# A weight ring of 16 units, a router by ranks among pairs, and a scatter in float32r halves

## The chip, the cores and the metric

The kernel runs on one core of a Trainium2 chip. The metric is the time of one execution on the device in microseconds (us); lower is better. Two kernels are compared by the medians of their runs.

## The reference

The program is a trunk of two post-norm layers on 256 tokens of width 1024. Each layer has a sub-layer of three parallel attention mixers and then a channel mixer: a dense SwiGLU in layer 0, and in layer 1 a mixture of eight experts of which each token uses two. The change is in layer 1's channel mixer:

```python
def swiglu(h, w_gate, w_up, w_down):
    return (jax.nn.silu(h @ w_gate) * (h @ w_up)) @ w_down

def moe_ffn(h, w_router, b_router, w_gate, w_up, w_down):
    """Top-2-of-8 SwiGLU experts; softmax over the two selected router logits."""
    B, S, D = h.shape
    hf = h.reshape(B * S, D)
    logits = (hf @ w_router).astype(jnp.float32) + b_router.astype(jnp.float32)
    top_v, top_i = lax.top_k(logits, TOP_K)
    top_w = jax.nn.softmax(top_v, axis=-1)
    combine = jnp.sum(jax.nn.one_hot(top_i, N_EXPERTS, dtype=jnp.float32) * top_w[..., None], axis=1)
    combine = combine.astype(h.dtype)
    out = jnp.zeros_like(hf)
    for e in range(N_EXPERTS):
        out = out + combine[:, e:e + 1] * swiglu(hf, w_gate[e], w_up[e], w_down[e])
    return out.reshape(B, S, D)
...
        h = layer_norm(ALPHA * h + y, ln_ffn_g[l], ln_ffn_b[l])
```

Everything is float32. D_FF is 3584, so an expert has three matrices of 1024 x 3584.

## The kernel before

**Weights as a stream of units.** All weights are laid out as units of 128 x 2048 float32 (1 MB). Layer 0 and 1 have 36 units each for the mixers, an expert (and the dense channel mixer) has 42. SyncE issues one load after another into a ring of slots, each when the unit that was in the slot has been used (semaphore `s_used`, counted up by TensorE at the last product of a unit). In the mixers and the dense part the ring has 7 slots (`raw_a`). In the expert part it has 14: `raw_a`, `raw_w` (one slot) and `raw_b` (six slots), whose space the mixers have used till then. `MOE_BASE` is the number of the first expert unit.

**Products in three parts.** Where many tokens are computed, a float32 product is made of three float32r products: ScalarE writes the unit's rounded copy `w_hi` (float32r), VectorE subtracts it from the unit (`w_lo`, called `lo_a`, `lo_b` and `lo_w` in the rows, in place of the raw unit), and TensorE adds up `x_hi w_hi + x_hi w_lo + x_lo w_hi` (L1530 to L1532). ScalarE and VectorE call this a split of the unit; three slots of `w_hi` are in use in the expert part. A unit needs twelve such products of 512 columns when 128 tokens are computed.

**Items.** The router lists items: an expert with up to 128 of its tokens (big, "B") or with up to 64 (small, "S"), in the order BSBSBSBS, so that experts with many tokens get the big ones. A small item takes full float32 products straight from the raw units (`x_small`, L1873 and L1907), with no split. The first seven items are written out, the eighth is the body of a loop that runs once or more often, where items overflow. Every item takes the 42 units in the order gate and up (groups of up to 1024 columns of D_FF) and down.

Each item goes like this on TensorE: the gate products of group 0 (four units); then `scatter` of the item before; up; group 1's gate; the transposes of the hidden values (L1880), and so on; near the end `gather` for the next item (L1836: 32 products that pick the tokens' columns of h by a one-hot matrix `gath`), and the last two down units. The result of an item stands in PSUM banks 4 and 5 (128 tokens x 1024). ScalarE and VectorE copy one half each to `d_sb`, four float32 products (L1847) with the transposed one-hot matrix `scat` place the rows at their tokens in banks 4 to 7, and VectorE multiplies by the router weight and adds to `cat`, which holds ALPHA * h (L1301).

**Order on an engine** is the order in which the code is written; every engine has its own instruction stream, with semaphores between them.

**The router.** After the last mixer's output h is normalised tile by tile (two tiles of 128 tokens; L1010 and L1015 are the last steps), each tile is transposed on TensorE (L1560), copied (`x_rt`), and multiplied with the router weights (L1959). `keep_warm(n)` puts n transposes of the identity matrix (L1566) on TensorE that nobody reads. VectorE finds the largest logit of each token, masks it, and finds the second (L1434 to L1446). TensorE counts ranks of tokens within experts with a triangular matrix (L1965 to L1969), VectorE makes the first gather matrix (L1312), and then the weights of the softmax, the lists of items and their overflow (L1456 to L1508). L987 are splits of units in the router's stretch, L1328 those of items.

## Time and profile before

| | us |
|---|---|
| median of 3 runs | 1654.53 (1654.35 to 1659.11) |
| the profiled execution, its own time | 1653.32 |
| its span, first to last instruction | 1651.5 |
| PE (TensorE) busy | 1557.0 (94%) |
| DVE (VectorE) busy | 963.3 (58%) |
| ACT (ScalarE) busy | 738.5 (45%) |

The mean granted TensorE clock was 0.973 of full speed. The mixers and the dense part fill the first 770 us, the router lies from 770 to 795, the eight items end at 1633, and the last normalisation and the stores of the output close the span. Durations of products overlap, since matmuls are pipelined: a product of 0.39 us can begin 0.23 us after the one before it. A row's time in the second place is that of a whole merged group where it has a count (x8).

### The profile page before, as it was taken

The page shows a single profiled execution, that of the slowest core. Times are in us where ns is not written, and L with a number is a line of the kernel's source. Part 1 is how long each engine was busy: PE and PEld are TensorE (multiplying, and loading weights), DVE is VectorE, ACT ScalarE, POOL GpSimd, SP SyncE. Part 2 cuts the span into 40 slices and gives each one's busy share as a digit, 9 for nine tenths or more (in the row PEclk, how much of TensorE's full clock was granted, in tenths as well). Part 3 has the DMA queues.
Part 4 walks back from the last instruction along what each step waited for, and adds up shares of the span by engine and source line. Part 5 has one row for each costly group of instructions (what it writes and reads, how often), then busy time and mean ns, then how long its engine had stood idle before and what let it go on. Part 6 is the DMA issues. An engine that isn't in the chain of part 4 may idle for free.

```text
span 1651.5 us, 18668 instructions
## 1 busy us (share of the span) xinstructions
PE 1557.0 (94%) x7600; PEld 1140.1 (69%) x7600; DVE 963.3 (58%) x904; ACT 738.5 (45%) x678; POOL 40.2 (2%) x30
## 2 busy tenths in 40 slices
PE   5999888999998999979899999999999999999996
PEld 3977777788886887867788436885368853688633
DVE  5547667455556546666899206993069930599403
ACT  3356654333433446653577105771057720477201
POOL 0000040000000000031000000000000000000000
PEclk9998989999999998989999999999999999999998
DMA  8353254455552452246699999999999999999994
GB/s 306 118 204 115 89 194 163 161 196 178 181 199 104 145 213 103 80 175 252 268 367 374 356 426 425 426 426 397 427 425 426 425 400 426 426 425 426 412 425 190
DMA packets 67013, 473.76 MB, mean 287 GB/s; under 512 B 8064, under 2 KB 8192, under 8 KB 10096
## 3 DMA queue, kind: packets, MB, share of 16 engines
q1 hardware_dynamic: 66096, 467.95, 70.9%
q0 software_dynamic: 832, 4.63, 0.8%
q8 instruction: 60, 0.98, 0.2%
q14 instruction: 25, 0.20, 0.0%
HBM read 471.50 MB, written 1.05 MB: 286 GB/s over the span
## 4 chain that ended last, share of the span: by engine, by line
PE 80%; DVE 9%; DMA 5%; ACT 3%; issue 2%; POOL 1%; SPq 0%; DVEq 0%; ACTq 0%; POOLq 0%
PE ps L1530 20%; PE ps L1531 19%; PE ps L1532 19%; PE ps L1873 11%; DMA raw_a<-in_w_item 4%; PE ps L1907 3%; DVE lo_a L987 2%; PE ps L1847 2%; PE ps L1836 1%; PE ps L1880 1%; ACT w_hi L662 1%; PE ps L1696 1%; PE ps L1560 1%; DMA raw_a<-in_w_mix 1%; DVE small L1003 1%
## 5 line engine op out<-in xcount | busy, mean ns | idle before, releaser
L987 DVE TENSOR_TENSOR lo_a<-raw_a,w_hi 128x2048 fp32r<-128x2048 f32 (+2 forms) x117 | 252.2, 2160 | 199.1 <-ACT w_hi L662 198.1
L662 ACT ACTIVATE w_hi<-raw_a 128x2048 fp32r<-128x2048 f32 (+2 forms) x117 | 209.5, 1796 | 180.0 <-PE ps L1532 174.5
L1530 PE MATMUL ps<-w_hi,act_hi 128*128 128x512 f32 (+1 forms) x640 | 254.8, 398 | 24.3 <-DVE act_lo L1053 11.4
L1531 PE MATMUL ps<-lo_a,act_hi 128*128 128x512 f32 (+1 forms) x640 | 249.8, 390 | 0.0
L1532 PE MATMUL ps<-w_hi,act_lo 128*128 128x512 f32 (+1 forms) x640 | 249.2, 389 | 0.0
L1328 DVE TENSOR_TENSOR lo_a<-raw_a,w_hi 128x2048 fp32r<-128x2048 f32 x81 | 184.3, 2289 | 19.7 <-ACT w_hi L898 18.8
L1530 PE MATMUL ps<-w_hi,x_hi 128*128 128x512 f32 x448 | 177.5, 396 | 9.0 <-DVE lo_a L1328 7.2
L898 ACT ACTIVATE w_hi<-raw_a 128x2048 fp32r<-128x2048 f32 x81 | 155.4, 1918 | 62.5 <-PE ps L1532 58.0
L1328 DVE TENSOR_TENSOR lo_b<-raw_b,w_hi 128x2048 fp32r<-128x2048 f32 x72 | 164.4, 2289 | 21.0 <-ACT w_hi L898 21.0
L1532 PE MATMUL ps<-w_hi,x_lo 128*128 128x512 f32 x448 | 174.6, 390 | 0.0
L898 ACT ACTIVATE w_hi<-raw_b 128x2048 fp32r<-128x2048 f32 x72 | 138.6, 1925 | 52.8 <-PE ps L1532 52.8
L1530 PEld LDWEIGHTS ps<-w_hi,act_hi 128*128 128x128 f32 x640 | 125.0, 195 | 53.3 <-DVE lo_a L987 8.6
L1532 PEld LDWEIGHTS ps<-w_hi,act_lo 128*128 128x128 f32 x640 | 125.0, 195 | 24.8
L1531 PEld LDWEIGHTS ps<-lo_a,act_hi 128*128 128x128 f32 x640 | 125.3, 196 | 22.8
L918 ACT ACTIVATE hidT<-ps 128x512 f32<-128x512 f32 (+1 forms) x16 | 8.7, 545 | 219.3 <-PE ps L1880 219.3
L1530 PEld LDWEIGHTS ps<-w_hi,x_hi 128*128 128x128 f32 x448 | 84.2, 188 | 30.8 <-issue 8.9
L1532 PEld LDWEIGHTS ps<-w_hi,x_lo 128*128 128x128 f32 x448 | 84.1, 188 | 18.2
L1873 PE MATMUL ps<-raw_a,x_small 128*64 128x512 f32 (+1 forms) x512 | 93.6, 515 | 0.0
L1530 PE MATMUL ps<-w_hi,hid_hi 128*128 128x512 f32 x224 | 87.6, 391 | 0.0
L1532 PE MATMUL ps<-w_hi,hid_lo 128*128 128x512 f32 x224 | 87.3, 390 | 0.0
L1338 DVE TENSOR_TENSOR sig<-ps,sig 128x512 f32<-128x512 f32 (+1 forms) x16 | 9.9, 619 | 128.6 <-ACT sig L909 128.6
L1873 PE MATMUL ps<-raw_b,x_small 128*64 128x512 f32 x384 | 84.6, 593 | 0.0
(254 smaller groups left out, 2228.9 us busy)
## 6 DMA issues: line engine op xcount, KB each, us to landing
raw_a<-in_w_item SPq DMA_DIRECT2D x210, 1024.0 KB, 11.4
raw_b<-in_w_item SPq DMA_DIRECT2D x144, 1024.0 KB, 14.7
raw_a<-in_w_mix SPq DMA_DIRECT2D x60, 1024.0 KB, 4.9
raw_w<-in_w_item SPq DMA_DIRECT2D x24, 1024.0 KB, 15.5
raw_a<-in_w_mix SPq DMA_DIRECT2D x8, 512.0 KB, 3.8
ln_gb<-in_ln_mix POOLq DMA_DIRECT2D x2, 1024.0 KB, 5.0
cst<-in_consts SPq DMA_DIRECT2D x1, 1178.0 KB, 20.1
h<-in_x SPq DMA_DIRECT2D x2, 512.0 KB, 8.0
```

Of the source, the lines that this page charges most:

```text
L662: nc.scalar.activation(w_hi[:, HI_SLOT[g], 0:n], raw(slot)[:, 0:n], ACT.Copy).then_inc(s_hi, 1)
L898: nc.scalar.activation(w_hi[:, it.hi_slot(k), :], raw(slot), ACT.Copy).then_inc(s_hi, 1)
L987: nc.vector.tensor_tensor(w_lo(slot)[:, 0:n], raw(slot)[:, 0:n], w_hi[:, HI_SLOT[g], 0:n].bitcast(F32), ALU.subtract).then_inc(s_lo, 1)
L1003: link(nc.vector.bn_stats(bst[:, t, b, :], src[:, t, 512 * b:512 * b + 512]))
L1328: nc.vector.tensor_tensor(w_lo(slot), raw(slot), w_hi[:, it.hi_slot(k), :].bitcast(F32), ALU.subtract).then_inc(s_lo, 1)
L1530: nc.tensor.matmul(dst, xh, wh, start=start, stop=False)
L1531: nc.tensor.matmul(dst, xh, wl, start=False, stop=False)
L1532: return nc.tensor.matmul(dst, xl, wh, start=False, stop=stop)
L1560: ins = nc.tensor.transpose(ps[:, bank, b * P:b * P + P], src[:, t, o:o + P], ident)
L1847: nc.tensor.matmul(ps[:, bank, :], scat[:, t, :], d_sb[:, 512 * half:512 * half + 512], start=True, stop=True).then_inc(s_cb, 1)
L1873: ins = nc.tensor.matmul(ps[64 * b:64 * b + 64, bank, 0:width // 2], x_small[:, kt, :], raw(slot)[:, o:o + width // 2], start=kt == 0, sto ...
L1907: ins = nc.tensor.matmul(ps[64 * half:64 * half + 64, 4 + half, :], hidT[:, b % (blocks // 2), a:a + 64], raw(slot)[:, o:o + 512], start=f ...
```

## The change

- **Ring.** `SLOTS` goes from 14 to 16: `raw_b` gets eight slots, counted down from the top of the memory, and their space comes from moving `cst`, `cat` and the small tiles. The load into the last slot waits for the last use of the layer-norm parameters `ln_gb`, which lie there. The looped eighth item uses 14 slots (`LOOP_SLOTS`).
- **Router.** The two largest logits are found by comparing all pairs: `ahead` counts for each expert how many logits are ahead of it, ties by the lower index; an expert is chosen if fewer than 2 are. The lists of items are made by operations over all values at once (`vals`, `tab`) and no longer one value at a time, in five pieces (`lists`) that stand between the splits of item 0. Two splits of units move from the router's chain to behind the gather matrix. The scaling of h into `cat` moves from VectorE to ScalarE. The first gather goes to banks 4 and 5, and item 0 begins its first products when the left half of the tokens is there.
- **Fillers.** `keep_warm` of 30 and 20 behind the two tiles become 14 and 8.
- **Scatter.** `d_sb` is replaced by `d_hi` (ScalarE, both halves, float32r) and `d_lo` (VectorE, the difference), and each bank is the sum of two float32r products.

```diff
-SLOTS_A, SLOTS = 7, 14
+SLOTS_A, SLOTS = 7, 16
+
+LOOP_SLOTS = 14
...
                     sp.wait_ge(s_used, MOE_BASE)
+                    if slot == SLOTS - 1:
+
+                        sp.wait_ge(s_lnd, 2 * DEPTH)
...
-                    hold(sp, s_used, j * ITEM_UNITS + (LOOP_BASE + k - SLOTS + 1))
+                    hold(sp, s_used, j * ITEM_UNITS + (LOOP_BASE + k - LOOP_SLOTS + 1))
...
-            def copy_down_left(it):
+            def copy_down_hi(it):
                 act.wait_ge(s_used, it.unit(ITEM_UNITS))
-                nc.scalar.activation(d_sb[:, 0:512], ps[:, 4, :], ACT.Copy).then_inc(s_dA, 1)
+                for half in range(2):
+                    nc.scalar.activation(d_hi[:, 512 * half:512 * half + 512], ps[:, 4 + half, :], ACT.Copy).then_inc(s_dA, 1)
...
             copy_tokens(0, True)
+            nc.scalar.activation(cat[:], h[:], ACT.Copy, scale=ALPHA).then_inc(s_res, 1)
...
                     norm(3, h, ln_gb, (s_gb, 48), adds, router_copy)
-                    split(nb + U_OUT + 5)
...
-            def copy_down_right(it):
-                dve.wait_ge(s_used, it.unit(ITEM_UNITS))
-                nc.vector.tensor_copy(d_sb[:, 512:1024], ps[:, 5, :]).then_inc(s_dV, 1)
+            def copy_down_lo(it):
+                for half in range(2):
+                    cols = slice(512 * half, 512 * half + 512)
+                    dve.wait_ge(s_dA, it.n * 2 + (half + 1))
+                    nc.vector.tensor_tensor(d_lo[:, cols], ps[:, 4 + half, :], d_hi[:, cols].bitcast(F32), ALU.subtract).then_inc(s_dV, 1)
...
-            first_largest(lg, m1, oh1)
-            link(nc.vector.scalar_tensor_tensor(lg2, oh1, -3e38, lg, ALU.mult, ALU.add))
-            first_largest(lg2, m2, oh2)
-            nc.vector.tensor_tensor(sel, oh1, oh2, ALU.add).then_inc(s_sel, 1)
-            nc.vector.tensor_tensor(dd, m2, m1, ALU.subtract).then_inc(s_rd, 1)
-            split(MOE_BASE + 2)
+            nc.vector.tensor_tensor(pair_gt, other, own, ALU.is_gt)
+            link(nc.vector.tensor_tensor(pair_eq, other, own, ALU.is_equal))
+            link(nc.vector.tensor_tensor(pair_eq, pair_eq, lower, ALU.mult))
+            link(nc.vector.tensor_tensor(pair_gt, pair_gt, pair_eq, ALU.add))
+            link(nc.vector.tensor_reduce(ahead, pair_gt, AX, ALU.add))
+            link(nc.vector.tensor_scalar(sel, ahead, 1.5, None, ALU.is_lt))
+            dve.sem_inc(s_sel, 1)
...
             link(nc.vector.tensor_tensor(rkm, ps[:, 6, 0:TILES * N_EXP].rearrange("p (t e) -> p t e", t=TILES), sel, ALU.mult))
-            link(nc.vector.tensor_scalar(rkm, rkm, -1.0, None, ALU.add))
             gather_matrix(lambda t: rkm[:, t, 0:1], True)
             nc.vector.tensor_copy(cnt, ps[:, 7, 0:N_EXP])
-            nc.vector.tensor_scalar(cat[:], h[:], ALPHA, None, ALU.mult)
...
+            split(MOE_BASE + 1)
             tokens_lo(0, None)
...
+            split(MOE_BASE + 2)
...
+            def by_position():
+
+                e688 = [P, 6, N_EXP, N_EXP]
+                each = prod.rearrange("p (r a b) -> p r a b", r=6, a=N_EXP)
+                link(nc.vector.tensor_tensor(each, at_pos.unsqueeze(1).to_broadcast(e688), vals.unsqueeze(2).to_broadcast(e688), ALU.mult))
+                link(nc.vector.tensor_reduce(tab[:, :, 0:N_EXP], each, AX, ALU.add))
...
-            item(Item(0), None, 3)
+            item(Item(0), None, 3, (weights, positions, by_position, overflow, overflow_items))
...
             def scatter(n):
 
-                pe.wait_ge(s_dA, n + 1)
-                pe.wait_ge(s_dV, n + 1)
                 pe.wait_ge(s_sTe, n + 1)
+
+                pe.wait_ge(s_dV, n * 2 + 2)
                 for q, bank in enumerate(SCATTER_BANKS):
                     t, half = q // 2, q % 2
-                    nc.tensor.matmul(ps[:, bank, :], scat[:, t, :], d_sb[:, 512 * half:512 * half + 512],
-                                     start=True, stop=True).then_inc(s_cb, 1)
+                    cols = slice(512 * half, 512 * half + 512)
+                    nc.tensor.matmul(ps[:, bank, :], scat[:, t, :], d_hi[:, cols], start=True, stop=False)
+                    nc.tensor.matmul(ps[:, bank, :], scat[:, t, :], d_lo[:, cols], start=False, stop=True).then_inc(s_cb, 1)
...
-                pe.wait_ge(s_xh, it.n * 2 + 2)
-                if it.big:
-                    pe.wait_ge(s_xl, it.bigs * 2 + 2)
-                project(0, GROUP_GATE[0], 0)
+                def gathered(b):
+                    pe.wait_ge(s_xh, it.n * 2 + b + 1)
+                    if it.big:
+                        pe.wait_ge(s_xl, it.bigs * 2 + b + 1)
+
+                first = before is None
+                gathered(0 if first else 1)
+                project(0, GROUP_GATE[0], 0, gathered if first else None)
...
-                keep_warm((30, 20)[t])
+                keep_warm((14, 8)[t])
```

The instruction order on TensorE (PE) from the first tile's router products to the first gather, before:

```order
L1959 MATMUL ps<-w_rt,x_rt 128x8 x8
L1566 MATMUL ps<-cst 128x128 x30
L1560 MATMUL ps<-cst,h 128x128 x8
L1959 MATMUL ps<-w_rt,x_rt 128x8 x8
L1566 MATMUL ps<-cst 128x128 x20
L1965 MATMUL ps<-rt,cst 128x8
```

The same place now, where L1619 is `keep_warm`, L1613 the transposes and L2019 the router products:

```order
L2019 MATMUL ps<-w_rt,x_rt 128x8 x8
L1619 MATMUL ps<-cst 128x128 x14
L1613 MATMUL ps<-cst,h 128x128 x8
L2019 MATMUL ps<-w_rt,x_rt 128x8 x8
L1619 MATMUL ps<-cst 128x128 x8
L2025 MATMUL ps<-rt,cst 128x8
```

The order is the same, and 16 and 12 fillers fewer stand behind the two tiles.

On VectorE (DVE), from the end of the choice of experts to the first work after the gather matrix (`gath`), before:

```order
L1446 TENSOR_TENSOR rt<-rt 128x16
L1447 TENSOR_TENSOR rt<-rt 128x2
L987 TENSOR_TENSOR lo_a<-raw_a,w_hi 128x2048
L1450 TENSOR_TENSOR rt<-ps,rt 128x16
L1451 TENSOR_SCALAR rt<-rt 128x16
L1312 TENSOR_SCALAR gath<-cst,rt 128x128 x2
L1453 COPY rt<-ps 128x8
L1454 TENSOR_SCALAR cat<-h 128x2048
```

And now (L1353 is the gather matrix, L1026 a split, L1369 an item's split, L1348 the second part of the gathered tokens):

```order
L1502 TENSOR_TENSOR rt<-rt 128x16
L1503 TENSOR_REDUCE rt<-rt 128x2
L1505 TENSOR_TENSOR rt<-ps,rt 128x16
L1353 TENSOR_SCALAR gath<-cst,rt 128x128 x2
L1507 COPY rt<-ps 128x8
L1026 TENSOR_TENSOR lo_a<-raw_a,w_hi 128x2048
L1348 TENSOR_TENSOR x_lo<-ps,x_hi 128x512 x2
L1026 TENSOR_TENSOR lo_a<-raw_a,w_hi 128x2048
L1369 TENSOR_TENSOR lo_a<-raw_a,w_hi 128x2048 x3
L1515 TENSOR_SCALAR rt<-rt 128x2
```

The splits stand behind the gather matrix, the scaling of `cat` is gone, and the first piece of the lists (from L1515) comes after three splits of the item.

On TensorE at the first scatter, that of item 0 within the small item 1, before:

```order
L1873 MATMUL ps<-raw_a,x_small 64x512 x16
L1847 MATMUL ps<-d_sb,scat 128x512 x4
L1873 MATMUL ps<-raw_a,x_small 64x512 x12
```

And now, with L1929 for the small item's products:

```order
L1929 MATMUL ps<-raw_b,x_small 64x512 x16
L1901 MATMUL ps<-d_hi,scat 128x512
L1902 MATMUL ps<-d_lo,scat 128x512
L1901 MATMUL ps<-d_hi,scat 128x512
L1902 MATMUL ps<-d_lo,scat 128x512
L1901 MATMUL ps<-d_hi,scat 128x512
L1902 MATMUL ps<-d_lo,scat 128x512
L1901 MATMUL ps<-d_hi,scat 128x512
L1902 MATMUL ps<-d_lo,scat 128x512
L1929 MATMUL ps<-raw_b,x_small 64x512 x8
```

Eight products stand where four stood, at the same place of the item; the unit ahead of them is in another slot of the ring.

## Rows read from the trace of the kernel before

**Rows 1.** The page: busy time and share of each engine.

```profile
PE 1557.0 (94%) x7600; PEld 1140.1 (69%) x7600; DVE 963.3 (58%) x904; ACT 738.5 (45%) x678; POOL 40.2 (2%) x30
```

**Rows 2.** Busy times by stretch, item 2 (big), item 3 (small); last clock, DMA share, GB/s.

```profile
1004.60:1121.10 116.50, 116.50 (x521) 94.90 (x521) 106.68 (x59) 83.39 (x50) 0.00 (x0) 1.00 1.01 426
...
1130.10:1211.00 80.90, 80.90 (x419) 32.29 (x420) 11.26 (x19) 7.16 (x13) 0.00 (x0) 1.00 1.00 416
```

**Rows 3.** Chain of waits, pieces in order of time: start, us, what.

```profile
1121.06 3.52 PE ps L1836 x32
...
1137.14 3.63 PE ps L1847 x8
...
1185.73 24.40 DMA raw_a<-in_w_item
...
1215.00 0.23 PE ps L1531
...
1225.70 3.43 PE ps L1847 x8
...
1424.71 0.47 PE ps L1530
```

**Rows 4.** Timeline at the start of item 4: start, us, instruction, [idle before].

```profile
1210.15 1.91 ACT L898 ACTIVATE w_hi<-raw_a 128x2048 fp32r<-128x2048 f32 x1 [0.39 <-DMA raw_a<-in_w_item]
...
1214.54 0.47 PE L1530 MATMUL ps<-w_hi,x_hi 128*128 128x512 f32 x1 [1.82 <-DVE lo_a L1328]
```

**Rows 5.** Timeline of SyncE's issues of loads around the router.

```profile
798.59 18.58 SPq L570 DMA_DIRECT2D raw_a<-in_w_item  x7
```

**Rows 6.** Timeline of TensorE in the router.

```profile
773.01 6.03 PE L1566 MATMUL ps<-cst 128*128 128x128 f32 x30
778.88 1.04 PE L1560 MATMUL ps<-cst,h 128*128 128x128 f32 x8
...
786.87 1.07 PE L1566 MATMUL ps<-cst 128*128 128x128 f32 x8
788.81 5.31 PE L1836 MATMUL ps<-gath,h 128*128 128x128 f32 x32 [0.87 <-DVE gath L1312]
795.59 0.47 PE L1530 MATMUL ps<-w_hi,x_hi 128*128 128x512 f32 x1 [1.46 <-ACT x_hi L883]
```

**Rows 7.** Timeline of VectorE in the router.

```profile
774.43 1.41 DVE L1015 SCALAR_TENSOR_TENSOR h<-h,small,ln_gb 128x512 f32<-128x512 f32 x2
...
782.97 0.18 DVE L1434 TENSOR_TENSOR rt<-ps,small 128x16 f32<-128x16 f32 x1
...
785.66 2.29 DVE L987 TENSOR_TENSOR lo_a<-raw_a,w_hi 128x2048 fp32r<-128x2048 f32 x1
787.86 0.17 DVE L1450 TENSOR_TENSOR rt<-ps,rt 128x16 f32<-128x16 f32 x1
...
788.28 0.48 DVE L1312 TENSOR_SCALAR gath<-cst,rt 128x128 f32<-128x128 f32 x2
...
803.17 0.17 DVE L1508 CAST itab<-rt 128x13 int32<-128x13 f32 x1
```

**Rows 8.** Timeline of VectorE in item 4: the split of unit 7.

```profile
1233.93 2.29 DVE L1328 TENSOR_TENSOR lo_w<-raw_w,w_hi 128x2048 fp32r<-128x2048 f32 x1
```

**Rows 9.** Timeline after the last item.

```profile
1632.79 0.60 ACT L876 ACTIVATE d_sb<-ps 128x512 f32<-128x512 f32 x1 [1.70 <-PE ps L1907]
...
1633.59 3.67 PE L1847 MATMUL ps<-d_sb,scat 128*128 128x512 f32 x8 [0.84 <-ACT d_sb L876]
1634.83 1.50 DVE L1301 SCALAR_TENSOR_TENSOR cat<-ps,rt,cat 128x512 f32<-128x512 f32 x2 [1.34 <-PE ps L1847]
1636.55 1.50 DVE L1301 SCALAR_TENSOR_TENSOR cat<-ps,rt,cat 128x512 f32<-128x512 f32 x2 [0.22 <-PE ps L1847]
```

**Rows 10.** Stretches of the router: length, busy times, granted clock, DMA share, GB/s.

```profile
774.00:776.00 2.00, 2.00 (x11) 2.00 (x10) 1.74 (x5) 0.00 (x0) 0.00 (x0) 0.50 1.02 430
788.50:792.00 3.50, 3.19 (x15) 3.19 (x16) 3.19 (x14) 0.00 (x0) 0.00 (x0) 0.51 0.37 152
```

255 lines of the change are left out of this document (139 added, 116 removed).

## The prediction

> **What bounds the kernel now.** I read the page first for the shares of the engines. TensorE is busy for 94% of the span, VectorE for 58% [rows 1], so the first question is what keeps TensorE's work as long as it is. The change works in the second half, in the router and the eight expert items. Two limits close together must be told apart, so I asked for the busy times of one big and one small item [rows 2]. The reader is to see that TensorE is busy in all 116.5 us of the big item and all 80.9 us of the small one, while the DMA engines are at a share of 1.0 too and move 426 and 416 GB/s.
>
> The chain of waits says which one holds [rows 3]. A pair of items (big and small) lies between the first products at 1214.54 [rows 4] and at 1424.71, so a pair takes 210.2 us. It has 84 weight units of 1.049 MB; at 426 GB/s a unit is 2.46 us and a pair 206.8 us. The chain runs over products of TensorE, and once in each pair over the landing of a load that was issued 24.4 us earlier. What that landing costs is in the timeline [rows 4]: ScalarE waited 0.39 us for the unit before it could split it, and TensorE stood still 1.82 us while ScalarE and VectorE split it. The other 1.4 us would be there with the unit landed long before. So TensorE's own work sets the pace, with the DMA 3 us behind it. A saved microsecond of TensorE work in an item is a saved microsecond of the kernel, until the DMA's limit is met.
>
> The second place is the router. The ring was full and the DMA ran dry soon after 788.5 [rows 10]; the next load was issued at 798.59, when TensorE had used its first expert unit [rows 5]. Everything between the end of the normalisation and the first expert product is a serial chain of small steps [rows 6, 7].
>
> **The change part by part.**
>
> *Router, on the path.* The second tile of h is normalised at 774.43 + 1.41 = 775.84 [rows 7], but its transposes began at 778.88: TensorE was in the 30 filler transposes, 6.03 us at 0.20 us each [rows 6]. With 14 they end at 773.01 + 2.8 = 775.8, which frees 3.0 us. The 8 real transposes, 1.04 us where they stood, now begin at the fillers' slow pace (8 x 0.20 = 1.6 us), so 0.6 goes back: **2.4 us**. The choice of two experts was 13 small operations, from 782.97 to the start of the next split at 785.66, 0.21 us each. It becomes seven, four of them on 128 elements instead of 16. Those have no row; the bounds are 0.17 us (16 elements) and 0.60 us (a quarter more than the 0.48 us that two 128-element operations took at 788.28). At about 0.35 us the chain is 2.1 us: **0.6 us**. The rank products were done when TensorE went on to 8 fillers at 786.87 [rows 6], but VectorE read them at 787.86, since it was in the split of 2.29 us that began at 785.66. That split and the one before it move behind the gather matrix, and one operation of 0.21 us goes, so the matrix is done 1.1 us earlier. The fillers end at 786.87 + 1.07 = 787.94, and the gather, which began at 788.81, can't start ahead of that: **0.8 us**. The first product waits for half of the gathered tokens instead of all. TensorE stood still 1.46 us before it [rows 6]; the left half was copied long before, so **1.4 us**. The sum is 5.2 us. The gather itself took 5.31 us here and 3.52 us in later items [rows 3, 6]; which it takes now depends on the clock, and I leave it at 5.31 with 1.8 us to either side.
>
> *Router, off the path.* The lists of items were some 40 operations in one run on VectorE up to 803.17, with item 0's splits behind it [rows 7]. SyncE's seven issues from 798.59, one for each unit that TensorE had used, spread over 18.6 us [rows 5] where six units need 16.6: 2.0 us lost. Now five pieces of 1 to 2 us (6.5 us in all) stand between the splits. A split is 2.29 us and a unit of TensorE twelve products 0.23 us apart [rows 3], 2.76 us, so VectorE has 0.47 us to spare for each unit; over the 20 units in question that is 9.4 us, and the sigmoids, hidden values and token copies there use about as much. I expect small stalls that add up to what is saved: 0 us, bounded by 2 us gained and 3 us lost. The scaled residual, 1.22 us on VectorE, goes to ScalarE, which waits for a ring slot then.
>
> *The ring of 16.* It takes effect in item 0: two more units land before TensorE needs a slot, and all later loads are issued two units earlier. In itself that gives nothing, since TensorE paces. It ends the wait of 0.39 us at each of three starts of a big item [rows 4], **1.0 us** with rounding down, and it is the cover for what follows: without it the faster TensorE would meet the DMA, 3 us behind, at once. The last item runs on 14 slots as before. The load of the ring's last slot waits for the last use of the layer-norm parameters at 775.84, when the queue still had work until about 790 [rows 10]: nothing.
>
> *The scatter.* Four full float32 products take 3.63 us in a small item and 3.43 us in a big one [rows 3]. They become eight float32r products. In the expert products such a product stands 0.23 us ahead of the next [rows 3], so eight take 1.84 us. Four small items gain 4 x 1.79 = **7.2 us**. Three big items would gain 1.59 us each, but VectorE caps that: after its four adds it splits unit 7, done at 1233.93 + 2.29 = 1236.2 [rows 8], and TensorE got to unit 7 at 1225.70 + 3.43 + 3 x 2.76 = 1237.4. Only 1.2 us can be had: **3.6 us**. The copies ahead of the scatter grow by 0.6 us on ScalarE and 0.7 us on VectorE; they lie beside four units of TensorE work (7.0 us in a small item, from its first product at 1130.1 [rows 2] to the scatter at 1137.14; 4 x 2.76 = 11.0 in a big one), and unit 3 behind them just arrives in time. Were that cover gone, each would cost 1.4 us.
>
> *The tail.* After the last item nothing covers the copies. Before, TensorE started 0.8 us after the end of the item and the first add at 2.04 us [rows 9]. Now two copies on ScalarE (1.2 us) and then one subtraction (0.7 us) precede it, so it starts at about 2.2 us, and the first add at about 2.9. The four adds run back to back in 3.0 us where they ended at 5.3: **0.7 us lost**.
>
> Sum: 5.2 + 0 + 1.0 + 7.2 + 3.6 - 0.7 = 16.3 us, so the span of 1651.5 becomes 1635.2, and the profiled execution's 1653.3 becomes 1637.0. Its time lies 1.2 us under the median of 1654.5; on the median's footing that is 1638.2, and I say **1638**.
>
> *The fillers, weighed.* The granted clock was 0.50 among the 30 fillers, the lower level of 1.2 GHz, and 0.51 in the 3.5 us at the start of the gather [rows 10], though 28 more fillers stood ahead of that. So the fillers did not hold the clock, and by the row I take nothing from their shortening. The Trainium skill, "TensorE: Matmul & The Clock Gate", section "HAM oscillation — how this bites in real kernels", says that an engine whose bursts are parted by waits falls back to the lower clock and pays for the warming again at each burst. By that rule the change, which takes 28 fillers out of 58, would lose speed in the gather and in the first expert units: the third rival below.
>
> **The rivals.**
>
> 1. *The DMA is the bound in small items.* There it moved 416 GB/s, not 426 [rows 2]: 42 x 2.46 + 42 x 2.52 = 209.2 us a pair. If that is what the DMA can do beside a small item, and not the sign of a nearly empty ring, the pair can't fall below 209.2. The gain is then the router's 5.2, two units of earlier loads (5.4) and the slack at the end: the last unit is used about 3 us after it lands. With 0.7 lost that is 12.9, or 1641.5. For it: the rate. Against it: the dip comes when the loads are issued shortest ahead of their landing, which 16 slots mend.
>
> 2. *A product of the scatter runs at the pace of full float32* (0.91 us, the 3.63 of [rows 3] over four), because its operands or the change of kind between neighbours ask for it. Then a scatter costs 7.3 us, 3.65 more than before, eight times: 29.2 us lost against 5.5 otherwise gained, or 1678. The eight scatters hold 64 products, so with the forecast's 16.3 the change turns from gain to loss above 0.23 + 16.3 / 64 = 0.48 us a product. Against it: the expert products of [rows 3] are of the same kind and size.
>
> 3. *The lower clock lasts through the router.* Gather 7.0 for 5.31 us (1.7 lost), the second tile's router products 0.8 us longer, and two expert units at double time (5.5): 8 us of the 16.3 lost, 1646. For it: two drops in this stretch already. Against it: the idle stretches between the bursts get shorter.
>
> 4. *VectorE absorbs the scatter's gain in the big items and the lists stall TensorE* (3.6 and 3 lost): 1645.
>
> **How the numbers follow.** A measurement tells about 0.3% (5 us) from no change. The forecast has 0.66, rival 1 0.17, rival 2 0.02, rivals 3 and 4 0.06 each, and 0.03 stays for what I have not seen, such as a drop of the clock in the mixers, which would hide the gain. The forecast's own range is 1634 to 1641: gather 1.8 either way, lists 2 to -3. To leave out no more than 2 in 10 I take **1633 to 1643.5**, which holds rival 1. Faster 0.95, same 0.03, slower 0.02.
>
> **What would show it.** The first expert product stands near 790 instead of 795.6. The second tile's transposes begin at about 775.9. The scatter's groups take 1.8 us and wait for no VectorE subtraction. The start of a big item idles 1.4 us, and a pair takes 206.5 to 207 us; 209 would mean rival 1. In item 0 VectorE shows stalls of TensorE of 2 to 3 us in all. The last adds start 2.9 us after the last unit. The prediction fails if the pair stays at 209 or more, or if the clock row of the router shows 0.5 beyond the gather.

## The result and the profile after

The changed kernel takes 1643.86 us (1640.74 to 1644.51, six runs), the kernel before 1654.44 us on the same chip; the ratio is 0.9938, 95% interval 0.9922 to 0.9955. The ratios in this document are to the kernel before, timed beside. The change gains 10.6 us where 16.3 were forecast, and the median lies 0.4 us above the stated range of 1633 to 1643.5. The profiled execution took 1641.09 us, 2.8 us under the median, with a span of 1639.3 us, 12.2 us less than the span before and 4.1 more than the 1635.2 forecast.

The page after, the row of [rows 1]:

```profile
PE 1543.1 (94%) x7572; PEld 1138.8 (69%) x7572; DVE 959.9 (59%) x883; ACT 743.1 (45%) x687; POOL 40.5 (2%) x30
```

Two pairs of items, busy times by stretch as in [rows 2]:

```profile
1001.90:1415.90 414.00, 410.81 (x1998) 270.48 (x1997) 245.08 (x165) 191.10 (x136) 0.00 (x0) 1.00 1.01 425
```

The chain of waits after, in the order of time, for [rows 3, 4]:

```profile
1012.15 0.94 DVE lo_b L1369
...
1014.36 1.22 DVE sig L1376
1015.58 2.63 DVE cat L1342 x4
1018.21 2.21 DVE lo_b L1369
...
1130.56 0.43 PE ps L1901
...
1132.63 13.88 PE ps L1929 x64
...
1205.89 0.47 PE ps L1583
...
1412.89 0.47 PE ps L1583
```

The scatter in the small item takes 1130.56 to 1132.63, 2.07 us for 3.63 before, and the small item's products follow at once. No landing of a load is in the chain between item 2 and item 4. From 1205.89 to 1412.89 a pair takes 207.0 us, for 210.2. The new piece is at the top: sigmoid, four adds and the split of unit 7 in one run of VectorE.

TensorE in the router, for [rows 6]:

```profile
775.10 3.23 PE L1619 MATMUL ps<-cst 128*128 128x128 f32 x14
778.12 1.92 PE L1613 MATMUL ps<-cst,h 128*128 128x128 f32 x8
780.91 1.92 PE L2019 MATMUL ps<-w_rt,x_rt 128*128 128x8 f32 x16 [0.88 <-DVE x_rt L1269]
782.69 1.07 PE L1619 MATMUL ps<-cst 128*128 128x128 f32 x8
784.86 0.60 PE L2025 MATMUL ps<-rt,cst 128*128 128x8 f32 x2 [1.10 <-DVEq L1497]
785.31 1.00 PE L2027 MATMUL ps<-rt,cst 128*128 128x8 f32 x4
786.16 1.00 PE L2029 MATMUL ps<-rt,cst 128*128 128x8 f32 x4
787.02 1.95 PE L1619 MATMUL ps<-cst 128*128 128x128 f32 x8
788.76 4.74 PE L1889 MATMUL ps<-gath,h 128*128 128x128 f32 x32
793.26 0.48 PE L1583 MATMUL ps<-w_hi,x_hi 128*128 128x512 f32 x1
```

The granted clock there (last but two in a row), for [rows 10]:

```profile
776.00:780.00 4.00, 4.00 (x19) 3.63 (x18) 1.91 (x6) 0.77 (x2) 0.00 (x0) 0.50 1.02 430
780.00:784.00 4.00, 2.88 (x25) 2.64 (x24) 1.83 (x8) 1.12 (x1) 0.00 (x0) 0.92 1.01 426
784.00:788.00 4.00, 3.14 (x15) 3.14 (x16) 2.31 (x13) 0.20 (x1) 0.00 (x0) 0.50 1.02 418
788.00:792.00 4.00, 4.00 (x26) 4.00 (x24) 2.17 (x1) 0.25 (x1) 0.00 (x0) 0.64 1.01 420
792.00:796.00 4.00, 4.00 (x26) 3.54 (x25) 2.52 (x3) 2.75 (x3) 0.00 (x0) 1.00 1.01 422
```

The clock was at its lower level (0.50) twice: around the transposes, which took 1.92 us for 1.04, and from the rank products into the gather, where it came back at about 791, before the gather's end. The 8 fillers behind the ranks ran at half speed too, 1.95 us for 1.07, and held the gather back. The gather matrix was done at 787.89 and the gather began at 788.76.

The end of the last item and the tail, timeline, for [rows 9]:

```profile
1608.37 1.94 PE L1963 MATMUL ps<-raw_a,hidT 128*64 128x512 f32 x8 [0.48 <-DMA raw_a<-in_w_item]
1610.80 1.94 PE L1963 MATMUL ps<-raw_a,hidT 128*64 128x512 f32 x8 [0.49 <-DMA raw_a<-in_w_item]
...
1620.26 1.08 ACT L913 ACTIVATE d_hi<-ps 128x512 fp32r<-128x512 f32 x2 [1.70 <-PE ps L1963]
1620.89 1.29 DVE L1333 TENSOR_TENSOR d_lo<-ps,d_hi 128x512 fp32r<-128x512 f32 x2 [16.30 <-ACT d_hi L913]
1622.23 0.50 PE L1901 MATMUL ps<-d_hi,scat 128*128 128x512 f32 x1 [2.02 <-DVE d_lo L1333]
...
1623.11 2.73 DVE L1342 SCALAR_TENSOR_TENSOR cat<-ps,rt,cat 128x512 f32<-128x512 f32 x4 [0.93 <-PE ps L1902]
```

TensorE now waits for loads in the last item, which it did not do before.

**Where the 12.2 us came from.** The trace records each time that TensorE counts a weight unit as used (`s_used`); "unit 3" below is the fourth of an item's 42, and the time of a unit runs from the count of the unit before it to its own. The differences of these times between the two profiled executions, unit by unit, give this ledger (positive is gained):

| | forecast | traces |
|---|---|---|
| start of the router's first transposes (768.0, now 770.1) | 0 | -2.1 |
| router, from there to the first unit used (30.5, now 26.1) | 5.2 | 4.4 |
| item 0: a stall at its unit 3 gone (4.65 to 2.72), two small ones new | 0 | 1.3 |
| small items' scatter, 4 x 1.57 | 7.2 | 6.3 |
| starts of big items (0.47, 0.50, 0.70) | 1.0 | 1.7 |
| big items' scatter, 4.8, less 1.9 of new stall at unit 7 and 0.2 elsewhere | 3.6 | 2.7 |
| last item's waits for loads | 0 | -1.7 |
| tail (18.8, now 19.1) | -0.7 | -0.3 |
| sum (the lines are rounded one by one) | 16.3 | 12.2 |

The first line isn't the change's doing: in the traces of both kernels and of all the variants the router begins somewhere from 767.8 to 771.9, by up to 4 us apart in kernels with the same code ahead of it. So a difference of 2 or 3 us between two medians of five or six runs is weak by itself, and the stretches of the traces, counted from the router's first transposes, weigh more. Without that line the change's own terms gain 14.3 us of 16.3.

### The profile page after: what moved, and what is told of

Same layout as the page of the kernel before. It is cut to its first block, busy times and chain, and to the rows that moved or that the text cites. A ratio compares the mean times of both kernels' runs of the same rounds, so it can differ in the third digit from the quotient of the medians.

```text
span 1639.3 us, 18611 instructions
## 1 busy us (share of the span) xinstructions
PE 1543.1 (94%) x7572; PEld 1138.8 (69%) x7572; DVE 959.9 (59%) x883; ACT 743.1 (45%) x687; POOL 40.5 (2%) x30
## 4 chain that ended last, share of the span: by engine, by line
PE 81%; DVE 10%; ACT 4%; issue 2%; DMA 2%; POOL 1%; SPq 0%; DVEq 0%; ACTq 0%
PE ps L1583 20%; PE ps L1584 19%; PE ps L1585 19%; PE ps L1929 11%; PE ps L1963 5%; PE ps L1889 2%; DVE lo_a L1026 2%; DMA raw_a<-in_w_item 1%; PE ps L1936 1%; ACT w_hi L698 1%; PE ps L1749 1%; PE ps L1613 1%; ACT w_hi L936 1%; DVE lo_b L1369 1%; DMA raw_a<-in_w_mix 1%
## 5 line engine op out<-in xcount | busy, mean ns | idle before, releaser
L1026 DVE TENSOR_TENSOR lo_a<-raw_a,w_hi 128x2048 fp32r<-128x2048 f32 (+2 forms) x117 | 251.2, 2151 | 198.7 <-ACT w_hi L698 197.7
L698 ACT ACTIVATE w_hi<-raw_a 128x2048 fp32r<-128x2048 f32 (+2 forms) x117 | 209.4, 1796 | 179.1 <-PE ps L1585 173.9
L1369 DVE TENSOR_TENSOR lo_b<-raw_b,w_hi 128x2048 fp32r<-128x2048 f32 x84 | 191.1, 2288 | 18.4 <-ACT w_hi L936 18.2
L936 ACT ACTIVATE w_hi<-raw_b 128x2048 fp32r<-128x2048 f32 x84 | 161.2, 1924 | 61.5 <-PE ps L1585 61.5
L1369 DVE TENSOR_TENSOR lo_a<-raw_a,w_hi 128x2048 fp32r<-128x2048 f32 x71 | 161.5, 2289 | 18.1 <-ACT w_hi L936 17.9
L936 ACT ACTIVATE w_hi<-raw_a 128x2048 fp32r<-128x2048 f32 x71 | 136.0, 1918 | 53.8 <-PE ps L1585 53.8
L1929 PE MATMUL ps<-raw_b,x_small 128*64 128x512 f32 (+1 forms) x528 | 99.7, 530 | 0.0
L1584 PE MATMUL ps<-lo_b,x_hi 128*128 128x512 f32 x224 | 87.9, 392 | 0.0
L1929 PE MATMUL ps<-raw_a,x_small 128*64 128x512 f32 (+1 forms) x440 | 87.3, 548 | 0.0
```

Source lines behind the costliest of these rows:

```text
L698: nc.scalar.activation(w_hi[:, HI_SLOT[g], 0:n], raw(slot)[:, 0:n], ACT.Copy).then_inc(s_hi, 1)
L936: nc.scalar.activation(w_hi[:, it.hi_slot(k), :], raw(slot), ACT.Copy).then_inc(s_hi, 1)
L1026: nc.vector.tensor_tensor(w_lo(slot)[:, 0:n], raw(slot)[:, 0:n], w_hi[:, HI_SLOT[g], 0:n].bitcast(F32), ALU.subtract).then_inc(s_lo, 1)
L1369: nc.vector.tensor_tensor(w_lo(slot), raw(slot), w_hi[:, it.hi_slot(k), :].bitcast(F32), ALU.subtract).then_inc(s_lo, 1)
L1584: nc.tensor.matmul(dst, xh, wl, start=False, stop=False)
L1929: ins = nc.tensor.matmul(ps[64 * b:64 * b + 64, bank, 0:width // 2], x_small[:, kt, :], raw(slot)[:, o:o + width // 2], start=kt == 0, sto ...
```

## The experiments

Two theories stood against each other for the router. **A**, the prediction's: fillers only delay what is queued behind them. **B**: they hold the clock, and fewer of them let it fall. For the items, theory one is that TensorE's own work paces them and the ring is the cover; its rivals are the DMA's rate and VectorE.

**The changed kernel again.** It was timed twice more, on other occasions, as the measure for the rest.

> The changed kernel as it is, for the same runs of the kernel before as the others of this set. Theory A (TensorE paces the items, the ring of 16 covers it, and only the eighth item starves at its end): a median of 1641 to 1644.5, a pair of items in 207.0 us, about 1.7 us of waits for loads in the last ten units. If the executions that are 3 us apart (1640.7 and 1641.1 against 1643.8 to 1644.5) are two courses of the router's clock, a further profile shows the first expert unit used at another time than 796.3, and the items behind it alike.

Measured: 1642.35 us (1639.93 to 1642.66, six runs), ratio 0.9913 (0.9887 to 0.994).

> The changed kernel once more, as the measure for the other two runs. 1641 to 1644 us. The router, from the first tile's transposes to the first product of the experts, 26 us in the executions near 1641 and 28 us in those near 1644.

Measured: 1641.29 us (1640.46 to 1643.51, six runs), ratio 0.9927 (0.9913 to 0.9941); its profiled execution took 1642.05 us. Both medians lie within their expectations, and inside the forecast's range: the result's own median missed it by less than this kernel's medians differ. They stay 3.1 and 4.2 us above the forecast's 1638.2. The items' times are equal to 0.1 us in the three traces of this kernel. The router isn't: 26.1, 26.2 and 28.6 us. In the last of them the clock row reads 0.50 all through:

```profile
776.00:780.00 4.00, 3.12 (x16) 2.75 (x14) 1.37 (x4) 1.88 (x2) 0.00 (x0) 0.50 1.01 426
780.00:784.00 4.00, 4.00 (x20) 4.00 (x20) 0.99 (x5) 0.00 (x0) 0.00 (x0) 0.50 1.01 420
784.00:788.00 4.00, 3.77 (x19) 3.37 (x18) 2.31 (x13) 0.20 (x1) 0.00 (x0) 0.50 1.01 422
788.00:792.00 4.00, 4.00 (x21) 4.00 (x20) 2.20 (x2) 0.00 (x0) 0.00 (x0) 0.50 1.02 426
```

So one and the same router costs 2.4 us more or less by the course of the clock. The expectation tied the long router to executions near 1644; this one took 1642.05, so the total doesn't tell which course a run took.

**Ring of 14.** `SLOTS_A, SLOTS = 7, 14`, all else as in the changed kernel.

> The changed kernel with the ring put back to 14 slots and all else kept. Theory A (the ring is the cover, and the dip of the DMA to 416 GB/s in the small items came from a nearly empty ring): the pair is held by the DMA at 209 to 210 us instead of 207.0, and two pairs and a half cost 5 to 8 us, so 1649 to 1652. Rival B (the dip belongs to the small items, whatever the ring, and TensorE has the pace at 14 as well): the pair stays near 207 and the time within 1.5 us of the changed kernel's.

Measured: 1646.05 us (1645.21 to 1648.74, eight runs), ratio 0.9937 (0.9915 to 0.9959); 3.7 us more than the changed kernel beside it, under the 5 to 8 expected and over the rival's 1.5. In its trace the later pairs take 209.4 and 209.0 us, as expected, and from the first unit used to the last the items take 5.7 us more. Its chain is back on a landing, and the timeline and the clock rows of the start of item 4 show what that costs:

```profile
1177.94 24.99 DMA raw_a<-in_w_item
...
1202.96 1.92 ACT w_hi L936
```

```profile
1207.34 0.47 PE L1583 MATMUL ps<-w_hi,x_hi 128*128 128x512 f32 x1 [2.41 <-DVE lo_a L1369]
```

```profile
1205.00:1209.00 4.00, 1.66 (x7) 1.39 (x8) 4.00 (x2) 3.25 (x2) 0.00 (x0) 0.95 1.01 424
1209.00:1212.00 3.00, 3.00 (x9) 2.33 (x8) 2.86 (x3) 1.74 (x4) 0.00 (x0) 0.50 1.01 429
1212.00:1215.00 3.00, 3.00 (x15) 2.45 (x14) 2.35 (x3) 1.96 (x2) 0.00 (x0) 1.00 1.03 434
```

TensorE waits 2.41 us where it waits 1.32 with 16 slots. Behind that gap the clock stands at 0.50 for 3 us (9 products in place of 15), so the start takes 6.8 us for 4.3: 1.1 us of waiting cost 2.5. The length of the gap doesn't decide it alone. At the start of item 6 of the same trace TensorE idles nearly as long, and the clock stays at 1.00:

```profile
1417.73 0.47 PE L1583 MATMUL ps<-w_hi,x_hi 128*128 128x512 f32 x1 [2.29 <-DVE lo_a L1369]
```

That start takes 5.3 us. The ring is what the forecast called it, the cover without which a part of the scatter's gain is lost again: 3.7 us of its 7.0 by the medians.

**Old scatter.** Four float32 products and the two old copies in the changed kernel.

```diff
-                nc.tensor.matmul(ps[:, bank, :], scat[:, t, :], d_hi[:, cols], start=True, stop=False)
-                nc.tensor.matmul(ps[:, bank, :], scat[:, t, :], d_lo[:, cols], start=False, stop=True).then_inc(s_cb, 1)
+                nc.tensor.matmul(ps[:, bank, :], scat[:, t, :], d_hi[:, cols], start=True, stop=True).then_inc(s_cb, 1)
```

> The changed kernel with the scatter as before: two copies on two engines and four full float32 products. Theory A: each small item gets 1.57 us back and each big one 1.0, 9.3 us in all, less 1.7 us since the eighth item would no longer wait for its loads, less 0.3 us at the tail: 7.3 us slower than the changed kernel, 1648 to 1652. Rival B (the DMA has the pace, and TensorE's saving was idle time elsewhere): at most 3 us slower.

Measured: 1649.31 us (1648.26 to 1650.63, twelve runs), ratio 0.9964 (0.9948 to 0.9981), 7.0 us more than the changed kernel. Its chain shows the scatter at 3.63 us, as before the change:

```profile
1134.16 3.63 PE ps L1899 x8
```

A pair takes 209.6 us, and the waits of the last item are gone: a slower TensorE doesn't catch up with the loads. The scatter's 9.0 us in the ledger are worth 7.0 net, as expected, since it brings the waits of the last item on itself.

**New scatter alone**, put into the kernel before, with its ring of 14 and its router.

> The kernel before with the scatter of the changed one alone; ring of 14, old router and fillers. Theory A: the pair is held by the DMA at 14 slots (209.0 and 209.4 us when only the ring was put back), so of 9.3 us only some 3 are left by the eighth item, and the kernel is 2 to 4 us faster than before. Rival (the scatter pays in full without the ring): 8 us faster.

Measured: 1651.09 us (1646.38 to 1653.12, twelve runs), ratio 0.9972 (0.9958 to 0.9985). In its trace the scatters gain as in the changed kernel (1.60 us in each small item). But the start of item 4 takes 6.87 us for 4.81, its wait for a landing followed by the same fall of the clock as with the ring of 14, and units 36 to 39 of the last item wait for loads, 2.5 us in all. Of the scatters' 9 us, 4.9 are left at the last unit. By the medians, beside 1653.42 for the kernel before, the gain is 2.3 us, within the 2 to 4 expected. TensorE idled for 2.29 us ahead of that fall.

**High half only.** The low half's product is left out, so that the output lacks the low part of each item's result; the copies stay.

> The changed kernel with the second product of each bank of the scatter left out: the low halves of the experts' outputs are not added, so the output lacks them; copies and waits stay. It takes 0.92 us of TensorE work out of each item. Theory A3 (at 2.48 us a unit the DMA needs 208.2 us a pair against TensorE's 207.0, and it is the ring's lead that pays the 1.2 us a pair; with TensorE at 205.2 it is used up in the second pair): the first pair takes 205.2 us, later ones 206 to 208, the eighth item waits longer for its loads, and the kernel gains 2 to 4 us of the 7.4 taken out. Rival (TensorE has the pace throughout): pairs of 205.2 to the end and 6.5 us or more gained.

Measured: 1640.76 us (1640.31 to 1643.39, six runs), ratio 0.9923 (0.9909 to 0.9936). Small items gain 0.92 us more, four products at 0.23. Big items gain 0.93 at the scatter and lose 0.90 at unit 7, which takes 4.21 us for 3.31. That is the cap by VectorE: units 4 and 7 together take 7.9 us in either trace, and two units without a scatter 5.5, so in a big item a scatter shorter than 2.4 us gains nothing.

The small items' 3.7 us didn't reach the end either: from the first unit used to the last, the trace is only 0.7 us shorter. Its pairs take 204.8, 206.0 and 207.1 us, so that nothing is left of the gain in the third, and three units of the last item wait 1.9 us more for loads. The reason can be read in both traces. In the changed kernel the first unit of items 2, 4 and 6 is used 11.8, 10.6 and 9.3 us after it landed, and here 10.8, 8.6 and 7.4. So the loads need 1.2 to 1.3 us more for a pair than TensorE's 207.0, some 208.2 as expected, and the ring's lead pays for it. TensorE has the pace, but with a lead that is being spent: the DMA is the next limit.

**Unit 7's split ahead of the adds.**

```diff
+                splits(7, 7)
                 if before is not None:
                     add_item(before.n, column(item_cw, before))
-                splits(7, 8)
+                splits(8, 8)
```

> The changed kernel, where VectorE splits unit 7 of a big item before it adds the scattered rows of the item before, and not behind the four adds. Theory A4 (in a big item VectorE takes back 0.6 to 0.7 us of the scatter's saving at unit 7, and took back all of it when the scatter was shorter still): unit 7 takes 2.75 us instead of 3.3 to 3.4 in items 2, 4 and 6, units 8 and 9 are not late in turn, a pair takes 206.4 us, 1.7 us gained in all, if the DMA lets it. Rival (the late unit 7 has another cause, or the stall moves to unit 8): the pair stays at 207.0.

Measured: 1644.41 us (1643.83 to 1645.56, six runs), ratio 0.994 (0.9926 to 0.9955): no gain where 1.7 us were expected. Unit 7 is 0.6 us shorter, and unit 8 is 1.3 to 1.5 us longer, 0.7 to 0.8 us lost in each of three big items. The wait has only moved:

```profile
1024.80 0.47 PE L1584 MATMUL ps<-w_hi,x_hi 128*128 128x512 f32 x1 [1.09 <-DVE lo_b L1369]
```

VectorE owes the same work at unit 8, and there TensorE meets it with less spare time.

**The last item's loads.** First, SyncE's eighth item written out, with the rule of 16 slots in place of 14 (the kernel then can't loop over further items).

> The changed kernel with SyncE's loads of the eighth item written out, by the ring's rule of 16 slots for its first 14 units and 14 behind them, and no loop for overflow items (this input has none, so it computes the same). Theory A: the DMA does not run nearly dry at units 13 and 14 of the eighth item, where it lost 3.8 us, its last landings come 3 to 4 us earlier, the waits for loads in the last ten units (1.7 us) go, and the kernel gains 1.5 to 1.9 us. Rival C (the two slow loads have another cause, such as the fetch of the loop's code): they stay at 3.4 and 5.3 us and nothing is gained.

Measured: 1640.98 us (1640.26 to 1644.08, six runs), ratio 0.9907 (0.988 to 0.9935). That is 1.4 us under the changed kernel beside it, near the 1.5 to 1.9 expected, but the trace doesn't bear it out: the last item is only 0.4 us shorter, 80.4 for 80.8. Two landings in its first units were still slow (3.03 and 4.26 us for 2.5). The trace shows what else moves there. GpSimd's load of the last layer-norm scale and shift, 1 MB broadcast to all partitions, is issued at 1537.80 by `pool.wait_ge(s_used, LOOP_BASE)`, in the middle of the weight stream. So second, that load put later:

```diff
-            pool.wait_ge(s_used, LOOP_BASE)
+            pool.wait_ge(s_used, LOOP_BASE + 40)
```

> The changed kernel, where GpSimd issues the last layer-norm parameters (1 MB, spread over the partitions) when unit 39 of the eighth item has been used, and not when the seventh item is done. Theory A2 (the eighth item's loads are late because the DMA has 43 MB to move in it and a dry stretch of 14 slots on top, and without the 43rd the last units land 2.5 us earlier): the 1.7 us of waits for loads before the last units go, the last unit is used 1.7 us earlier against the first of the eighth item, and the kernel is 1.5 to 2 us faster than the changed one. Rival (the slow landings at units 13 and 14 of the eighth item alone are the cause, and the parameters ride in a gap): no change beyond 0.5 us.

Measured: 1641.57 us (1639.71 to 1642.76, five runs), ratio 0.9922 (0.9907 to 0.9937). The last item takes 79.1 us for 80.8, and TensorE's units at the end follow without a gap:

```profile
1606.59 3.60 PE L1963 MATMUL ps<-raw_b,hidT 128*64 128x512 f32 x16
1610.03 3.60 PE L1963 MATMUL ps<-raw_a,hidT 128*64 128x512 f32 x16
```

The 1.7 us are all there in the last item. They aren't all there at the end: the tail took 19.8 us for 19.1. The clock fell during its scatter, whose products stand 0.43 us apart where most of them stood 0.23 apart. The tail of the last version below took 19.9 us too, but so did, to 0.2 us, the tails of two traces with the early load (ring of 14, unit 7's split ahead), so no run tells whether the late load brings it about. The late load is worth 0.9 us in this trace, and 1.7 without that fall. This trace's router also took 27.5 us, with the clock at 0.50 from 777 to 794.

**Fillers.** First the old numbers in the changed kernel, `keep_warm((30, 20)[t])`:

> The changed kernel with the fillers of before: 30 and 20 behind the two tiles of the router instead of 14 and 8. Theory A (fillers cost time only where they outlast the normalisation, and do not hold the clock): the second tile's transposes begin 3 us later at the full clock, so the first expert unit is used 2.4 us later, counted from the first tile's transposes: 28.6 instead of 26.2 us. Rival 3 of the prediction (they hold the clock): the course of 28.7 us with the clock low for 20 us, seen in the kernel with the ring of 14, does not come up, the runs lie closer together, and the median is no worse than the changed kernel's.

Measured: 1638.64 us (1637.49 to 1640.77, five runs), ratio 0.991 (0.9895 to 0.9926). The router takes 25.5 us, the shortest of all traces, though 28 more fillers stand in it. Theory A had expected 28.6.

```profile
776.00:780.00 4.00, 3.92 (x25) 3.68 (x23) 0.04 (x1) 0.48 (x1) 0.00 (x0) 0.69 1.01 422
780.00:784.00 4.00, 3.20 (x29) 3.23 (x30) 1.90 (x8) 1.40 (x2) 0.00 (x0) 1.00 1.01 428
784.00:788.00 4.00, 4.00 (x37) 3.86 (x36) 3.33 (x13) 0.20 (x1) 0.00 (x0) 1.00 1.01 418
788.00:792.00 4.00, 4.00 (x31) 3.75 (x31) 2.40 (x4) 1.90 (x3) 0.00 (x0) 1.00 1.02 426
```

```profile
785.45 0.59 PE L2029 MATMUL ps<-rt,cst 128*128 128x8 f32 x4
785.90 1.07 PE L1619 MATMUL ps<-cst 128*128 128x128 f32 x8
786.83 3.84 PE L1889 MATMUL ps<-gath,h 128*128 128x128 f32 x32
```

The clock comes back within the 30 fillers and stays at 1.00: the gather takes 3.84 us for 4.74. And it isn't this trace alone. Each execution's mean granted clock is on record: with 30 and 20 it is 0.972 to 0.974 in all five, and 0.966 to 0.969 in all 17 executions of the three kernels with 14 and 8 or none on the same chip. Then none at all, behind the ranks neither:

> The changed kernel with no fillers at all in the router (30 fewer than its own). Theory A: the first gather begins when its matrix is ready, 0.9 us earlier, and nothing else moves: 25.3 us from the first tile's transposes to the first unit's use, and the kernel 0.9 us faster. Rival 3 (the waits between bursts let the clock fall and each burst pays): the clock is at 0.5 through the router and the first units, 3 to 8 us lost.

Measured: 1643.53 us (1640.88 to 1643.92, six runs), ratio 0.9933 (0.992 to 0.9947), 4.9 us more than with 30 and 20 on the same chip. The routers of the two traces differ by less, 27.1 us for 25.5; the profiled one here began 4.0 us later, and that can't be the fillers' doing. Theory A had 25.3 for this router. Its clock row reads 0.50 from the transposes to the gather:

```profile
781.00:785.00 4.00, 3.12 (x15) 2.99 (x15) 0.80 (x3) 1.25 (x1) 0.00 (x0) 0.50 1.01 426
785.00:789.00 4.00, 1.97 (x10) 1.87 (x10) 2.58 (x12) 0.20 (x1) 0.00 (x0) 0.50 1.01 416
789.00:793.00 4.00, 3.21 (x15) 3.12 (x15) 2.93 (x5) 0.00 (x0) 0.00 (x0) 0.50 1.02 424
```

Then 20 behind each tile:

> The changed kernel with 20 and 20 fillers instead of 14 and 8. Theory F (it is the busy TensorE between the router's steps that brings the clock back to 1.0 by the second tile's products; with 14 and 8 it came back late, by a second drop or a low stretch of 17 to 20 us, with 30 and 20 at once): with 20 the fillers end near the end of the normalisation, and the router takes 24 to 25.5 us if the clock comes back, 27 to 29 if not. Rival (only the length behind the second tile counts): the same as with 30 and 20, less 2 us.

Measured: 1638.45 us (1638.02 to 1640.46, five runs), ratio 0.9905 (0.9889 to 0.9921). The profiled execution was the slowest of the five; its router took 26.0 us, between the 24 to 25.5 expected if the clock came back and the 27 to 29 if not. It came back and fell once more, from 784 to 787. The mean clock of the five was 0.970 or 0.971.

Last, the edit of the fillers alone in the kernel before, `keep_warm((14, 8)[t])`:

> The kernel before with one edit: 14 and 8 filler products instead of 30 and 20. Theory A (the prediction's step): the queue is 2.4 us shorter, the second tile's transposes start 3.0 us earlier and nothing else moves: 2 to 2.5 us faster than the kernel before. Theory B (the fillers hold the clock): the transposes start earlier, but the clock row shows 0.5 through the rank products and the start of the gather, each product there lasts 1.7 times as long, and the kernel is level to 2 us slower than before: the first expert product comes no earlier, counted from the first tile's transposes.

Measured: 1652.8 us (1648.96 to 1657.67, twelve runs) against 1654.37, ratio 0.9994 (0.9981 to 1.0007): no difference that the runs can tell. The interval still admits A's 2.4 us; the router in the trace doesn't. The transposes begin where the 14 fillers end, as A has it, but they run at the low clock, and after a stretch at 1.00 the ranks and the gather do again:

```profile
779.23 1.91 PE L1560 MATMUL ps<-cst,h 128*128 128x128 f32 x8
...
787.40 1.00 PE L1967 MATMUL ps<-rt,cst 128*128 128x8 f32 x4
...
790.84 5.72 PE L1836 MATMUL ps<-gath,h 128*128 128x128 f32 x32
```

```profile
780.00:784.00 4.00, 3.13 (x24) 2.75 (x23) 2.82 (x2) 1.88 (x2) 0.00 (x0) 0.83 1.01 426
```

The router takes 29.9 us for 30.5: 0.7 us of the 2.4 are left. The clock is low there for 17 us in all, for 10 in the kernel before, and the mean clock of the twelve executions is 0.968 to 0.973, for 0.971 to 0.975. Another 1.4 us were gained in this trace at the starts of items 2, 4 and 6 (4.28, 4.31 and 4.56 us for 4.74, 4.81 and 5.01), which neither theory has.

**Together.** First 30 and 20 fillers, the late load and unit 7's split ahead of the adds:

> The changed kernel with three edits that the runs so far speak for: 30 and 20 fillers, the last layer-norm parameters loaded when unit 39 of the eighth item has been used, and unit 7 split ahead of the adds. By the single effects: 3 to 4 us from the clock, 1.7 from the parameters, up to 1.7 from unit 7, of which the DMA's 208.2 us a pair may take a part: a median of 1634 to 1637, against 1638.6 with the fillers alone.

Measured: 1641.43 us (1640.89 to 1645.38, six runs), ratio 0.9926 (0.991 to 0.9942). That missed the 1634 to 1637 expected. The order of the splits cost its 0.7 us three times, as above, and the clock fell a second time in the profiled execution, one of two near 1645, in spite of the 50 fillers; its router took 30.3 us. Then 20 and 20 fillers and the late load, with the splits left alone:

> The changed kernel with 20 and 20 fillers and with GpSimd's load of the last scale put behind 40 more units. Theory B: the two gains add, since they lie 800 us apart: 3 us from the router and 1.7 us from the last item's loads, so 1637 us, 4.5 us faster than the changed kernel beside it. Theory A: the fillers give back nothing and cost some 1 us: 1642 us.

Measured: 1637.88 us (1637.36 to 1639.15, five runs), ratio 0.9904 (0.9888 to 0.9919), 3.4 us faster than the changed kernel beside it, with 4.5 expected; the last item takes 79.1 us again, the tail 19.9. All five executions are faster than all six of the changed kernel. It is the fastest version found.

## Why the prediction was partly right

**The step that failed is "The fillers, weighed".** It took 2.4 us from the shorter queue and nothing for the clock, since the rows of before showed a low clock in spite of 58 fillers [rows 10]. The row was read rightly and carried too far: that the clock falls with fillers doesn't show that it would stay up as well with fewer. In before it was low for 7 us and then for 3; in the changed kernel for 7 and 7, or for 20 at a stretch. The longer fillers beat the 14 and 8 by medians each time: by 1.7 us (20 and 20, the late load's 1.7 taken off), 1.3 (30 and 20 in the version with three edits against the one with the splits alone, 1.7 taken off), and 2.9, or 4.6 with the late load's 1.7 put back (30 and 20 against the late load alone). If the late load is worth only 0.9, these are 2.5, 2.1 and 3.8. In the traces one router with 30 and 20 is 0.6 to 3.1 us shorter than those with 14 and 8 (the other took 30.3 us). So the term of +2.4 was worth +0.7 in the router of the kernel before, and in the changed kernel it is a loss, of 0.6 to 4.6 us by these measures.

By the Trainium skill, "TensorE: Matmul & The Clock Gate", section "HAM oscillation — how this bites in real kernels", bursts parted by waits start cold each time. The rows here agree in part: without fillers the clock was at 0.50 from 777 to 794; with 30 and 20 it was back at 1.00 from 779 on in one trace, and in the other it fell again at 783. Rival 3 had the mechanism right. Its size was too large: 8 us, since it put the low clock into the first expert units, which ran at full speed in every trace. Neither sign that was to refute the forecast came. The pair took 207.0 us and not 209, and the clock was back at 1.00 before the gather's end, with no 0.5 beyond it. The loss lay at the ranks and in the gather's first half, where the prediction had set no sign.

**The router's terms one by one.** The shorter queue gave 2.0 us for 2.4: the transposes began 2.9 us earlier and ran 0.9 longer. The choice of experts took 1.9 us (782.87 to 784.75) for 2.7, a gain of 0.8 for 0.6. The term for ranks and gather matrix was +0.8 and came out at -0.9, since the rank products and the 8 fillers behind them ran at half speed. The first product no longer waited for the right half, 1.7 us for 1.4. The gather gained 0.6 and small differences 0.2. With 5.2 forecast and 4.4 found the sum looks nearly right, but it holds a gather that was faster than before by the luck of the clock, 4.74 for 5.31.

**The mis-sized terms.** The small scatter gained 1.57 us for 1.79: seven products follow 0.23 us apart, as taken from [rows 3], and the first takes 0.43. The starts of big items gained 1.7 us in all for 1.0. These can't be put down to the ring alone: 1.4 of them came in the kernel before too, when only its fillers were shortened, and the cause of that is open. The cap by VectorE was right in place and kind, with 0.9 net for 1.2 in each big item; the run with the high half only shows it. Item 0 gained 1.3 us for 0: before, TensorE had stood still at unit 3 for a split that VectorE owed behind the old unbroken run of list operations, and that unit took 1.9 us more. The tail lost 0.3 for 0.7.

**The term that was missing** is the last item, 1.7 us. "The last item runs on 14 slots as before" costed its loads at nothing, with TensorE some 12 us earlier. Before, unit 36 of the last item was used 4.5 us after its landing. With TensorE ahead by 14 us and the landings by 12 to 13, 2.4 were left, and the next three units waited. The 14 slots are a small part (0.4 us); the scale's megabyte beside the weights is the larger, though it stood there in the kernel before too.

**Rival 1** is refuted: the small items' 416 GB/s was the nearly empty ring. With 16 slots a pair takes 207.0 us, and 425 GB/s hold over two pairs. (Its 5.4 us for two units of earlier loads should have been 2 x 2.46 = 4.9.) **Rival 2** is refuted by the 0.23 us a product. **Rival 4** is right in neither half: the lists stalled TensorE by 0.5 us in item 0 and not by 3, and 2.7 of the big items' 3.6 us stayed.

What isn't settled is why the clock takes one course or the other in executions of one kernel. Over the nine profiled executions with 14 and 8 fillers in the changed router, the router took from 26.1 to 28.6 us. With 30 and 20 it took 25.5 once and 30.3 once, so more fillers make the good course likelier and don't ensure it.

Nor do the terms account for all of the shortfall of 5.7 us against 1638.2. The ledger gives 2.0 of it, and the later start 2.1 in the profiled execution. The other 1.6 is that execution's place 2.8 us under the median, where 1.2 had been allowed for. The longer course of the router, 2.4 us, would fit, but no trace of those slower executions shows it.

## What to carry to other kernels

Before you take out work that nobody reads, ask what it holds up: price its removal with the engine at its lower clock in the short steps that follow, and keep the difference in the range. When the bounding engine becomes faster, walk the loads to the very end of the stream, other engines' loads included, and see where the slack between landing and use runs out. A stall taken from one unit of a saturated engine comes back at the next, so moving it is no gain unless the engine behind it gets less to do.

## What the runs showed of the hardware

A wait can cost more than its length. At the start of item 4, TensorE idle for 1.32 us was followed by a granted clock of 1.00, idle for 2.41 us by 0.50 for 3 us; the second start took 2.5 us longer, of which 1.1 are the wait. It needn't: idle for 2.29 us at the start of item 6 of the same trace, and for 2.34 us with the high half only, it went on at 1.00, while 2.29 us in the kernel before with the new scatter were followed by 0.50. Four float32 products of 128 x 512 took 3.63 us and eight float32r ones 2.07, so splitting an operand in two float32r parts more than paid for the second product. And a megabyte by GpSimd's queue beside a weight stream of 425 GB/s showed up not where it was moved but 70 us later, as two waits at the end of the item.
